# Routing worked out with one partition per expert, the conditioning vector turned by TensorE, and the S5 output matrices loaded in whole pieces

## The reference

```
h  = rms_norm(x) * (1 + scale1) + shift1
q, k, v, u = split(h @ W_in)
x  = x + gate1 * (concat[diff_attention(q, k, v), s5_mixer(u)] @ W_out)
h2 = rms_norm(x) * (1 + scale2) + shift2
x  = x + gate2 * moe(h2)
```

## Time and profile before

| what | value |
|---|---|
| median of 3 runs | 1717.65 us (1715.22 to 1718.13) |
| the profiled execution's own time | 1717.55 us |
| its span, first to last instruction | 1715.8 us |
| mean granted TensorE clock | 0.91 of full |
| busy: PE, DVE, POOL, ACT | 1479.8, 778.3, 530.9, 302.9 us |
| moved by DMA | 493.23 MB, mean 287 GB/s |
| instructions | 48747 |

### The profile page before, as it was taken

How to read it: one execution, slowest core, us unless ns; L and a number is a source line. 1 busy time by engine, 2 the same in 40 slices (tenths; PEclk the granted TensorE clock), 3 DMA queues, 4 the chain that set the end, 5 groups by cost and what they waited for, 6 DMA issues and landing times.

```text
span 1715.8 us, 48747 instructions
## 1 busy us (share of the span) xinstructions
PE 1479.8 (86%) x19899; PEld 840.4 (49%) x19899; DVE 778.3 (45%) x1872; ACT 302.9 (18%) x844; POOL 530.9 (31%) x533
## 2 busy tenths in 40 slices
PE   4899998999749999999989998999798898797690
PEld 2356555465435555455545454555354454353240
DVE  3857466642574344343434343443333342342235
ACT  4222275532201111011111111111010010110000
POOL 3085999227012232232223132222221221221110
PEclk8997999989859999999999899999898898898785
DMA  9432234873773942949697999999999999999976
GB/s 270 161 49 49 65 71 121 293 219 96 284 266 102 408 156 72 408 159 397 260 406 263 409 360 363 388 374 408 408 408 408 409 408 408 408 408 408 407 294 246
DMA packets 141927, 493.23 MB, mean 287 GB/s; under 512 B 20764, under 2 KB 25156, under 8 KB 137764
## 3 DMA queue, kind: packets, MB, share of 16 engines
q1 hardware_dynamic: 128976, 469.60, 72.7%
q0 software_dynamic: 8416, 16.98, 2.8%
q10 hardware_dynamic: 4432, 5.25, 0.9%
HBM read 474.18 MB, written 17.84 MB: 287 GB/s over the span
## 4 chain that ended last, share of the span: by engine, by line
PE 54%; DMA 23%; SPq 14%; DVE 5%; issue 2%; ACT 2%; ACTq 0%; DVEq 0%; POOLq 0%; POOL 0%
PE bank L1801 31%; DMA w_ring<-mlp_w 17%; SPq L427 13%; PE bank L1518 5%; PE bank L1681 3%; PE bank L1606 2%; DMA ada_slab<-ada_w 2%; DMA ada_half<-ada_w 2%; PE bank L1510 2%; PE bank L1820 1%; PE bank L1793 1%; PE bank L1615 1%; PE bank L1781 1%; DVE final_acc L1433 1%; PE bank L1710 1%
## 5 line engine op out<-in xcount | busy, mean ns | idle before, releaser
L1801 PE MATMUL bank<-w_ring,xs_T 128*32 128x256 f32 x10240 | 617.4, 394 | 47.6 <-DMA w_ring<-mlp_w 47.6
L1801 PEld LDWEIGHTS bank<-w_ring,xs_T 128*32 128x32 f32 x10240 | 333.4, 113 | 294.4 <-DMA w_ring<-mlp_w 77.1
L651 POOL DMA_INDIRECT xs<-h_rows,row_idx x82 | 188.5, 2299 | 781.3 <-DVE row_idx L1361 734.4
L1801 PE MATMUL bank<-w_ring,act_T 128*32 128x256 f32 x5120 | 340.6, 404 | 59.9 <-DMA w_ring<-mlp_w 59.9
L1801 PEld LDWEIGHTS bank<-w_ring,act_T 128*32 128x32 f32 x5120 | 154.6, 114 | 178.3 <-DMA w_ring<-mlp_w 58.6
L1379 DVE TENSOR_SCALAR glu<-bank 128x128 f32<-128x128 f32 x160 | 46.6, 291 | 387.2 <-PE bank L1801 379.3
L953 DVE TENSOR_TENSOR slot_onehot<-iota_slots,slots 128x2048 bf16<-128x2048 f32 x83 | 189.3, 2281 | 0.0
L930 ACT ACTIVATE sigmoid<-glu 128x128 f32<-128x128 f32 x160 | 48.9, 305 | 540.7 <-DVE glu L1379 466.3
L934 ACT ACTIVATE act_T<-bank 128x128 f32<-128x128 f32 x160 | 44.3, 277 | 499.0 <-PE bank L1820 499.0
L672 POOL DMA_INDIRECT ys_rows<-y_rows_sb,row_idx x80 | 82.1, 1027 | 147.4 <-DVE y_rows_sb L953 143.4
L1356 DVE TENSOR_REDUCE row_idx_f<-bank 128x1 f32<-128x3 f32 x82 | 13.1, 160 | 211.3 <-PE bank L1781 211.3
(11 more groups left out here) (337 smaller groups left out, 1543.9 us busy)
## 6 DMA issues: line engine op xcount, KB each, us to landing
w_ring<-mlp_w SPq DMA_DIRECT2D x384, 1024.0 KB
ada_half<-ada_w SPq DMA_DIRECT2D x16, 1024.0 KB, 5.6
dense_ring<-w_in SPq DMA_DIRECT2D x4, 2048.0 KB, 13.7
final_rows<-ys_rows SPq DMA_DIRECT2D x4, 2048.0 KB, 14.7
dense_ring<-ada_w SPq DMA_DIRECT2D x3, 2048.0 KB, 28.9
x_all<-x SPq DMA_DIRECT2D x2, 1024.0 KB, 14.3
ada_slab<-ada_w SPq DMA_DIRECT2D x1, 2048.0 KB, 39.7
state_ir<-state_ri SPq DMA_DIRECT2D x4, 512.0 KB, 5.3
```

Source lines behind the costliest of these rows:

```text
L651: pool.indirect_dma_start(out=xs[:], out_offset=None, in_=h2_v, in_offset=bass.IndirectOffsetOnAxis(ap=idx[:, 0:1], axis=0), bounds_check= ...
L1801: last = mm(bk[BLK * j:BLK * j + BLK, 0:ZW], x(h0 + i), w[:, i, ZW * j:ZW * j + ZW], start=False, stop=(stop and i == 1))
```

## The change

- c is loaded as 8 rows of 128 numbers, and PE turns it into bank 7, from which ACT and DVE read it. `pe_prep` counts one more step.
- The S5 output matrices are loaded into a tile of their own, `cnat`, in pieces of 8 x 64 numbers, 2 KB, per partition; POOL makes three copies of it into `CC` instead of one.
- The gate row's quarters are loaded behind the modulation rows, in the middle of the kernel; DVE's wait for them moves from ahead of the loop to ahead of the second norm. `g2q` and `ysb` trade places.
- The squares of `x1_squares` go to bank 7; the wait for the store and turn of tile t - 2 moves to DVE, into `norm_rows`, ahead of h2.
- The ordering of the experts has one expert per partition: keys and counts come as a column, comparisons are 32 x 32 in all, and what has to be a row on all partitions is made by PE from small products. The counts against the block thresholds, first blocks and ends follow in the same way. `order_matrices` is gone. `mask_ready` becomes `route_in`, which counts the hand-overs to PE; `blocks_ready` counts the list and the ends only.
- `block_ends` moves from behind slots(2) to behind slots(1), ahead of rows(1). On PE x_turn(1) moves ahead of rows(2). On ACT the wait for the ends moves behind x_out(1).

```
@@ start
-            act.dma_start(ccol[:, 0, :], I["c"][0].rearrange("(t p) -> p t", p=P)).then_inc(s["c_loaded"], 16)
+            act.dma_start(crow[:], I["c"][0].rearrange("(t p) -> t p", p=P)).then_inc(s["c_loaded"], 16)
-                act.dma_start(CC[:, :, k, :], I[n][0].rearrange("d g c p -> (d g c) p")
+                act.dma_start(cnat[:, k], I[n][0].rearrange("d g c p -> (d g c) p")
                               .rearrange("(q t) p -> q t p", t=8)).then_inc(s["s5_nat"], 16)
-            act.wait_ge(s["c_loaded"], 16)
-            act.activation(ccol[:, 1, :], ccol[:, 0, :], ACT.Sigmoid).then_inc(s["lam_e"], 1)
+            act.wait_ge(s["pe_prep"], 1)
+            act.activation(ccol[:, 1, :], bank[7][:, 0:KT], ACT.Sigmoid).then_inc(s["lam_e"], 1)
-            pool.tensor_copy(CC[:, :, 2, :], CC[:, :, 0, :]).then_inc(s["nat_dup"], 1)
+            for k, part in ((0, 0), (1, 1), (2, 0)):
+                pool.tensor_copy(CC[:, :, k, :], cnat[:, part]).then_inc(s["nat_dup"], 1)
+            pe.wait_ge(s["c_loaded"], 16)
+            tr(bank[7][:, 0:KT], crow[:], ident[0:KT, 0:KT]).then_inc(s["pe_prep"], 1)
...
@@ SP
             sp.dma_start(mod[:, 1:4]...)
+            for j in range(TILES):
+                sp.dma_start(g2q[BLK * j:BLK * j + BLK], dram["mod_rows"][0, 3 * D + ZW * j:3 * D + ZW * j + ZW]
+                             .partition_broadcast(BLK)).then_inc(s["mod_loaded"], 16)
             sp.wait_ge(s["y_mm"], 4)
...
-            sp.wait_ge(s["blocks_ready"], 3)
-            for j in range(TILES):
-                sp.dma_start(g2q[...])
+            sp.wait_ge(s["blocks_ready"], 2)
...
@@ x1_squares, norm_rows
-                if t >= 2:
-                    act.wait_ge(s[f"h2_stored{t % 2}"], 16 * (t // 2))
-                    act.wait_ge(s["h2_tr"], t - 1)
                 for k in range(2):
-                    ch.free(act.activation(h2[:, t % 2, 512 * k:512 * k + 512], x1[:, t, 512 * k:512 * k + 512],
+                    ch(act.activation(bank[7][:], x1[:, t, 512 * k:512 * k + 512],
                                            ACT.Square, accum_out=sq_s[:, 5 * t + k:5 * t + k + 1]))
...
+                if t >= 2:
+                    dve.wait_ge(s[f"h2_stored{t % 2}"], 16 * (t // 2))
+                    dve.wait_ge(s["h2_tr"], t - 1)
                 ch(dve.scalar_tensor_tensor(h2[:, t % 2], x1[:, t], SQ(t, 4), mod[:, 2], ALU.mult, ALU.mult))
...
@@ DVE, routing: new
+                ch.free(dve.scalar_tensor_tensor(COL(0), bank[7][0:E, 7 * E:7 * E + 1], float(E), pm[0:E, 0:1], ALU.mult, ALU.subtract))
+                ch(dve.scalar_tensor_tensor(keyr[:], bank[7][0:E, 6 * E:7 * E], float(E), iotaE[0:E, :], ALU.mult, ALU.subtract))
+                ch(dve.tensor_scalar(cmpc[:], keyr[:], COL(0), None, ALU.is_lt))
+                ch(dve.tensor_reduce(COL(1), cmpc[:, FIXED:E], AX.X, ALU.add))
+                ch.free(dve.tensor_scalar(COL(2), COL(1), 2.0, float(FIXED), ALU.mult, ALU.add))
+                ch(dve.tensor_scalar(COL(3), COL(1), -2.0, 2.0 * E - 1.0 - FIXED, ALU.mult, ALU.add))
+                ch(tt(COL(4), COL(2), COL(3), ALU.min))
+                ch(dve.tensor_copy(col[0:FIXED, 4:5], pm[0:FIXED, 0:1]))
+                dve.tensor_copy(posB[:], COL(4).to_broadcast([E, E])).then_inc(s["route_in"], 1)
+                dve.tensor_scalar(ordm[:], iotaE[0:E, :], COL(4), None, ALU.is_equal).then_inc(s["route_in"], 1)
+
+            def list_experts():
+                dve.wait_ge(s["part_mm"], 3)
+                dve.tensor_copy(eat[:], bank[1][:, 0:E]).then_inc(s["blocks_ready"], 1)
+                ch(dve.tensor_copy(eatf[:], bank[1][:, 0:E]))
+                ch(dve.tensor_scalar(lessT[:], bank[0][0:E, 0:E], COL(4), None, ALU.is_gt))
...
             dve.wait_ge(s["pos_mm"], 1)
+            ch(dve.tensor_copy(COL(5), bank[2][0:E, 0:1]))
+            ch(dve.tensor_scalar(cmpt[:], thr[0:E, :], COL(5), None, ALU.is_lt))
+            ch(dve.tensor_reduce(COL(6), cmpt[:], AX.X, ALU.add))
+            ch(dve.tensor_scalar(COL(7), COL(6), 1.0, None, ALU.max))
+            dve.tensor_copy(nbB[:], COL(7).to_broadcast([E, P])).then_inc(s["route_in"], 1)
+            dve.wait_ge(s["pos_mm"], 2)
+            ch(dve.tensor_copy(COL(8), bank[0][0:E, E:E + 1]))
+            dve.tensor_scalar(endB[:], COL(7).to_broadcast([E, P]), COL(8), None, ALU.add).then_inc(s["route_in"], 1)
+            ch(dve.tensor_copy(rt[:, 0, :], bank[0][:, 0:E]))
+            ch(dve.scalar_tensor_tensor(slotE[:], bc(rt[:, 0, :], 1, NT, [P, NT, E]), float(BLK),
+                                        bank[7][:, 0:NT * E].rearrange("p (t e) -> p t e", e=E), ALU.mult, ALU.add))
...
@@ DVE, order of the steps ahead of the loop
             slots(1)
+            block_ends()
             rows(1)
...
             slots(2)
-            block_ends()
             rows(2)
...
-            dve.wait_ge(s["mod_loaded"], 32 + 64)
             dve.sem_inc(s["y2_ev"], 1)
...
@@ PE
+            pe.wait_ge(s["m_sq"], NT)
             for q in range(NT - 1):
-                last = mm(bank[7][:, 6 * E:7 * E], onb[:], mask[:, q, :], start=(q == 0), stop=(q == NT - 2))
+                mm(bank[7][0:E, 6 * E:7 * E], onb[:, 0:E], mask[:, q, :], start=(q == 0), stop=(q == NT - 2))
+            for q in range(NT - 1):
+                last = mm(bank[7][0:E, 7 * E:7 * E + 1], mask[:, q, :], onb[:, 0:1], start=(q == 0), stop=(q == NT - 2))
             last.then_inc(s["part_mm"], 1)
             router(3)
...
+            mm(bank[0][0:E, 0:E], posB[:], ident[0:E, 0:E], start=True, stop=True).then_inc(s["part_mm"], 1)
+            pe.wait_ge(s["route_in"], NT + 1)
+            mm(bank[1][:, 0:E], eB[:], ordm[:], start=True, stop=True).then_inc(s["part_mm"], 1)
...
+            pe.wait_ge(s["route_in"], NT + 3)
+            mm(bank[0][0:E, E:E + 1], lessT[:], nbB[:, 0:1], start=True, stop=True)
+            mm(bank[0][:, 0:E], nbB[:], lessT[:], start=True, stop=True).then_inc(s["pos_mm"], 1)
+            pe.wait_ge(s["route_in"], NT + 4)
+            mm(bank[1][:, 0:E], endB[:], ordm[:], start=True, stop=True).then_inc(s["pos_mm"], 1)
...
             rows(1)
+            x_turn(1)
             rows(2)
-            x_turn(1)
```

104 lines of the change are left out of this document (44 added, 60 removed).

## The result

The changed kernel takes 1705.34 us (median of 5 runs, 1701.02 to 1707.48), the kernel before 1715.22 (5 runs, 1711.41 to 1718.13). The ratio is 0.9936, 95% interval 0.9912 to 0.9960, which is 6.9 to 15.1 us off. The profiled execution took 1705.34 us, with a span of 1703.6. The forecast was 1707.0, range 1701.2 to 1711.8.

What follows compares the result with a forecast made beforehand. No one engine bounds the kernel; the expert loop is a chain hung on its own start. 1.2 + 2.7 + 2.7 + 2.9 + 1.0 = 10.5 us off 1717.55 gives 1707.0 us, range 1701.2 to 1711.8.

Steps and rivals of the forecast that it cites:

- the start: First 60 us: fewer small pieces on the shared DMA engines let x and the ada slab land 1.2 us earlier.
- the norm: Four row tiles: ScalarE's squares of tile 2 no longer wait for tile 0's store; 2.7 us.
- ordering ahead of the last choice: Routing on VectorE: ten small operations replace the old ordering, so the last mask comes 2.7 us earlier.
- last mask to slot one-hot: Routing's second half: the path of 7.53 us becomes 4.65, a gain of 2.9 us.
- the first block: First expert block: 2.3 us gate wait back, less 1.2 for the second gather and 0.2; with hand-overs 1.0 us.
- The routing: Expert ordering and slots made narrow: 2.7 us ahead of the last mask and 2.9 us behind it.
- the new wait for the second gather: First expert block: PE waits 1.2 us at x_turn(2), as rows(2) now stands behind x_turn(1).
- Rival (a): The start gives nothing: pieces go out unmerged, or x is slowed by its own writes; 1708.2 us, chance 0.09.
- The gate row: Its four loads issued earlier at no cost, ending PE's 2.30 us idle time in the first expert block.
- (c): Expert loop: the weight stream is the bound, an earlier first block only fills the ring; about 1716, chance 0.10.
- (d): Expert loop gets slower: PE waits for gathers, 0.3 us in some 50 blocks, 15 us lost; 1722, chance 0.06.
- (b): Routers: TensorE keeps its full clock through them, giving 5.3 us more speed; 1701.7 us, chance 0.07.

Runs made afterwards that it cites:

- late_12: Changed kernel with VectorE's sum of the slots done 13 times instead of once, delaying the first slot one-hot: 1712.96 us, ratio 0.9978.
- warm_all: Changed kernel with the second row sum ahead of the first gathered tile's turn, and unread products filling TensorE's idle time around routers and gather: 1701.41 us, ratio 0.9920.
- The repeat: Changed kernel run and profiled again, nothing edited: 1708.67 us, ratio 0.9948 against the kernel before.
- warm_more: Like warm_all, but 5 fp32 fillers instead of 7 behind the second router, and more bf16 fillers, also between the routing products: 1702.46 us, ratio 0.9939.
- gate_late: Changed kernel with the gate row's four loads back behind the block counts, as before the change: 1712.74 us, ratio 0.9985.
- late_at_52: Changed kernel with ACT's small evacuation of the modulation columns done 17 times instead of once, at 52.7 us: 1711.12 us, ratio 0.9971.

## Why the prediction was right, and where it was off

The forecast was right in direction, in range and in most terms. Term by term, measured from the landmarks:

| step | forecast | measured |
|---|---|---|
| the start | 1.2 | 0.65 at x, 0.44 at the slab (not clear of spread), nothing seen from 55 us on |
| the norm | 2.7 | 2.9 at the first row sum (2.66 at the second block) |
| ordering ahead of the last choice | 2.7 | 2.73 |
| last mask to slot one-hot | 2.9 | 2.72 |
| the first block | 1.0 | -0.1 |
| sum | 10.5 | 8.2, and 0 to 0.65 of the start |

- **The norm** was read rightly: what came late next was PE, with mix(3) and router(0), and VectorE's choice behind it. PE's turn of tile 3 stands 25.65 us behind S instead of 28.59.
- **The routing** was read rightly in both halves. The ten operations took 1.66 us instead of the 2.1 forecast, which changed nothing, since PE was late next. The Trainium skill's page "VectorE: DVE Perf Modes" (The TRN2 errata) would have made one such operation 0.09 us. The rows have 0.13 to 0.23 us, so they side with the forecast; the page itself says that this row of its table under-predicts single operations. The 1.8 us that the prediction drew from it is too much in any case: ten of its 18 operations run in VectorE's wait for router(3), so only the eight behind the last mask could have gained. (The items of the second half add up to 4.61 us, not 4.65; measured were 4.81.)
- **The first block** is the step that failed in size. The steps were right: the gate's 2.3 us came back, and the new wait for the second gather came, 1.49 to 1.64 us instead of 1.2. What was left out were two prices: the first gather reached PE 9.98 us behind the row sum instead of 9.52 (means of the two profiles of each kernel), and the first up product took 5.2 us instead of 4.82, at a mean granted clock of 0.68 and 0.71 instead of 0.75 and 0.74. That the step's low end was -0.2 kept it inside the forecast. Why the first gather got slower wasn't tried. The profiles have an order: from its issue to PE's turn it took 7.7 to 8.1 us where it was issued 8 to 10 us behind the first of the nine weight pieces (nine profiles), 7.5 to 7.8 at 12.4 us (four), and 7.4 at 16.7 us (late_12). That would fit the gather sharing the DMA engines with those pieces, but it isn't shown.
- **The start** was too high. Rival (a), that it gives nothing, described the outcome better than the forecast's own term, though its reason was wrong: the pieces did go out merged, and x did land earlier. The term read the load of the small pieces as time on the critical transfer; of 1.2 us the slab got 0.44 in the mean, against a spread of 2 us from one execution to the next. Where the rest went between the queues stays open.
- **The gate row** was booked as 2.3 us of the first block. As a sum that is right, since before and after are what they are; as the worth of the part it is wrong. With the norm and the routing in place, the early load is worth 6.9 us, and those two without it 1.4 instead of 8.2.
- **The head carries the loop**: what reaches the second block reaches the end, by the slope of 0.96 over twelve kernels and by the rest in late_12, and that ruled out (c). A shift ahead of the first block need not arrive whole: of late_12's 8.65 us, 6.4 did. (d) is out by the waits of the loop. (b) was out in the change itself, routers 1 to 3 took 3.62 us; warm_all shows that the rival's price was real, yet smaller: 2.3 us at the row sum, not 5.3, since router(1) and most of router(2) lie beside VectorE's work.

SP resumed at 539.82, not at 536.9: 1.1 us of that are the first block, the rest is the start and where S fell (0.72 us later than before). That the time came out 1.7 us below the forecast all the same is the rest of that execution, 4.6 us shorter than in the profile of before. The repeat (7.1 us between medians, 8.9 by the ratio) fits the 8.2 us of the rows better. The base was high as well: over 17 to 35 runs each, the kernel before has medians of 1713.18 to 1716.74 us, not 1717.55. So the predicted time owes some of its closeness to luck.

## What to carry to other kernels

When a chain is shortened ahead of a transfer that sits behind a full queue, first ask where that transfer's landing is set: by the chain or by the bytes ahead of it. Here moving four small loads decided whether 8 us of faster norm and routing arrived or 1.4. Read the worth of a part between fixed landmarks, not between two end times: these repeat within 0.1 to 0.4 us while the time of one kernel spreads over 10. And where small products alternate with waits, price TensorE's work at the clock of the rows around it; filling a wait paid here only where the clock was still up and the filler ended before the work it stood ahead of.

## What the runs showed of the hardware

- Where TensorE idled between small products, the work behind paid for it. The first up product, behind the wait for the gather, took 4.75 to 6.04 us in fourteen profiles, against 3.62 us for the next one of the same size. With fillers of 128x512 in fp32 around the routers the granted clock stayed at 1.00 from 456 to 480 us (warm_all). In warm_more TensorE idled 3.02 us behind a stretch at 1.00, and from 496 to 500 us the mean was 0.53. The Trainium skill's page "TensorE: Matmul & The Clock Gate" (Part 1) makes the clock follow how busy the engine was of late, and the rows agree with that.
- A load of 256 KB cut from 256-byte to 2 KB pieces landed in 2.7 and 3.0 us (the two loads) instead of 3.9 and 4.2, yet the transfer that the start waits for gained no more than 0.44 us in the mean, which isn't clear of its spread: the time that small pieces took on one queue was not given whole to another.
- Issuing takes longer behind other issues: the four gate loads took SP 4.82 us to issue when they came 12.5 us behind the first of nine weight pieces (gate_late), against 1.73 us at 17.0 us behind it in the kernel before; the DMA engines were full both times. What sets it isn't shown.
- Four small loads behind nine of 1 MB on the same queue were there 30.7 to 31.1 us behind the issue of the first of the nine, whether they were issued 12.5 or 17.0 us behind it (four profiles of three kernels, by the end of VectorE's wait).
- Most of the spread comes from outside the edited middle: 8 us at S (late_at_52 apart) and 11 us in the rest over all profiles, with DMA-paced waits in both.
